# The twelve conditioning chunks of the input stage, computed on VectorE with features on partitions instead of as matrix products on TensorE

## The reference, cut to what matters

```python
# first block, D_MODEL = 1024
sh1, sc1, gt1, sh2, sc2, gt2 = split(silu(c) @ ada_w + ada_b, 6)       # ada_w: 1024 x 6144
csh1, csc1, ...              = split(silu(c_ctx) @ ada_w + ada_b, 6)   # only csh1 and csc1 are used
h = rms_norm(x) * (1 + sc1) + sh1
q, k, v, g, hy_u, gate_ret, gate_hy = split(h @ w_in + b_in)           # w_in: 1024 x 6656
...
# second block, two layers, conditions c_2 and c_ctx_2, ada_w_2: 2 x 1024 x 6144
m = silu(cond) @ ada_w_2[layer] + ada_b_2[layer]
```

## Time and profile before

| what | us |
|---|---|
| median of 3 runs | 1832.39 |
| lowest and highest run | 1829.98, 1832.53 |
| span of the profiled execution | 1829.5 |
| TensorE busy in the span | 1767.4 |
| VectorE busy in the span | 462.7 |

### The profile page before, as it was taken

One profiled execution on the slowest core, in us unless ns is written; L12 is line 12 of the kernel. 1 busy time (PEld: TensorE's weight loads), 2 busy tenths in 40 slices (PEclk: granted clock), 3 DMA queues, 4 the chain that ended last, 5 costly groups with the idle time before them and its releaser, 6 DMA issues. The chain is left out here.

```text
span 1829.5 us, 24606 instructions
## 1 busy us (share of the span) xinstructions
PE 1767.4 (97%) x10866; PEld 1344.7 (73%) x10866; DVE 462.7 (25%) x1010; ACT 324.7 (18%) x732; POOL 0.2 (0%) x4
## 2 busy tenths in 40 slices
PE   6999999999999999999999999999999999999997
PEld 4674887888664466676667577688888876888886
DVE  5310124525125221111101144531100135411001
ACT  4110013103214111010000123521100125211000
POOL 0000000000000000000000000000000000000000
PEclk9999999999999999999999999999999999999999
DMA  9453677467999999999999973365444331554430
GB/s 380 177 224 116 259 316 280 185 253 268 372 391 414 401 421 420 421 421 421 398 421 407 421 291 118 139 241 181 153 161 140 113 116 46 215 200 161 142 111 23
DMA packets 61810, 472.93 MB, mean 259 GB/s; under 512 B 7719, under 2 KB 11208, under 8 KB 12040
## 3 DMA queue, kind: packets, MB, share of 16 engines
q1 hardware_dynamic: 60472, 470.08, 65.7%
q10 hardware_dynamic: 1232, 1.28, 0.2%
HBM read 470.29 MB, written 1.05 MB: 258 GB/s over the span
## 5 line engine op out<-in xcount | busy, mean ns | idle before, releaser
L2520 PE MATMUL bank<-hT,ring 128*128 128x256 f32 x1024 | 221.5, 379 | 0.0
L2539 PE MATMUL bank<-second_work,ring 128*128 128x256 f32 x1024 | 221.3, 379 | 0.0
L2539 PEld LDWEIGHTS bank<-second_work,ring 128*128 128x128 f32 x1024 | 194.6, 190 | 26.5
L2520 PEld LDWEIGHTS bank<-hT,ring 128*128 128x128 f32 x1024 | 194.4, 190 | 26.4
L1345 PE MATMUL bank<-hT,ring 128*128 128x256 f32 x704 | 160.8, 385 | 4.5 <-issue 2.7
L1345 PEld LDWEIGHTS bank<-hT,ring 128*128 128x128 f32 x704 | 133.1, 192 | 39.8 <-issue 12.9
L650 PE MATMUL bank<-hT,ring 128*128 128x256 f32 x704 | 153.9, 379 | 0.0
L650 PEld LDWEIGHTS bank<-hT,ring 128*128 128x128 f32 x704 | 133.5, 191 | 18.8 <-issue 1.2
L1813 PE MATMUL bank<-ring,rowsT 128*32 128x512 f32 x1008 | 117.5, 597 | 1.2 <-DMA ring<-in_expert_w 1.0
L1345 PE MATMUL bank<-tmp,ring 128*128 128x256 f32 x384 | 86.5, 382 | 5.9 <-DMA ring<-in_w_out 4.3
L1345 PEld LDWEIGHTS bank<-tmp,ring 128*128 128x128 f32 x384 | 71.9, 190 | 24.8 <-DMA ring<-in_w_out 7.8
(11 more groups left out here) (468 smaller groups left out, 1707.5 us busy)
## 6 DMA issues: line engine op xcount, KB each, us to landing
ring<-in_expert_w SPq DMA_DIRECT2D x190, 1024.0 KB, 12.2
ring<-in_w_ff SPq DMA_DIRECT2D x96, 1024.0 KB, 7.1
ring<-in_ada_w SPq DMA_DIRECT2D x36, 2048.0 KB, 10.4
ring<-in_w_in SPq DMA_DIRECT2D x29, 1024.0 KB, 8.2
ring<-in_w_in SPq DMA_DIRECT2D x13, 2048.0 KB, 8.8
ring<-in_w_out SPq DMA_DIRECT2D x12, 1024.0 KB, 6.0
ring<-in_ret_w_o SPq DMA_DIRECT2D x2, 2048.0 KB, 8.2
ring<-in_w_out SPq DMA_DIRECT2D x2, 2048.0 KB, 12.8
```

The costliest lines, as they stand in the source:

```text
L2520: mm = pe.matmul(ff_bank(n), w[:, k, (n % 2) * P:(n % 2 + 1) * P], hT[:, k, xs], start=k == 0, stop=k == DT - 1)
L2539: mm = pe.matmul(ff_bank(FT + i), w[:, f, :], W[:, 16 * h + f, :], start=h == f == 0, stop=h == 1 and f == FT // 2 - 1)
```

## The change

The 12 conditioning chunks of the input stage leave TensorE. The host lays their weights out transposed (`rows_first`): a chunk holds 4 groups of 128 output features, the features on the partitions, the 1024 input features along the row; it is still 128 x 4096. The conditions come as rows, broadcast to all partitions by three transfers of 128 x 1024 on SyncE's queue, ahead of `early` and the chunks, and ScalarE takes their silu behind tile 9. One step of `weigh` is a `scalar_tensor_tensor` on VectorE over 128 x 1024: weights times condition, with the sum along the row written to `mod`. A0 to A3 are now the chunks of `mods[2]`, with two conditions, 8 steps each; A4 to A11 are those of `mods[0]`, with one condition, 4 steps each: 64 steps. The steps are spread over the tiles of the projection chunk that comes next in the list, behind that tile's evacuation where VectorE does it. A conditioning chunk is released by its last step. The conditioning chunks also move in the list: the counts behind each projection chunk change from 0 0 1 1 1 1 1 1 2 1 1 1 1 to 0 1 1 1 2 2 1 1 1 1 1 0 0.

```diff
-                  [wide("ada_w", j) for j in range(ADA0, 12)] + [wide("ada_w_2", j, 1) for j in range(4)],
-                  [0, 0, 1, 1, 1, 1, 1, 1, 2, 1, 1, 1, 1])
+                  [features_first("ada_wT", j) if l is None else features_first("ada_wT_2", j) for l, j in ROW_CHUNKS],
+                  [0, 1, 1, 1, 2, 2, 1, 1, 1, 1, 1, 0, 0])
...
+                    cond_rows = {0: row_of(tmp[:, 6:8, :]), 2: row_of(gates[:, 12:16, :]), 3: row_of(tmp[:, 0:2, :])}
+                    products_out = row_of(tmp[:, 2:4, :])
+                    row_jobs = [(c, mods[0], 4 * (ADA0 + j), (0,)) if l is None else (c, mods[2], 4 * j, (2, 3))
+                                for c, (l, j) in zip(at["in_beside"], ROW_CHUNKS)]
+                    row_steps = [(n, i, m) for n, job in enumerate(row_jobs) for i in range(4) for m in range(len(job[3]))]
...
+                    def row_steps_after(i):
+
+                        here = [s for s, (n, _, _) in enumerate(row_steps) if i in tiles_of_next[n]]
+                        if not here:
+                            return range(0)
+                        where = tiles_of_next[row_steps[here[0]][0]]
+                        done = lambda t: here[0] + len(here) * t // len(where)
+                        return range(done(where.index(i)), done(where.index(i) + 1))
+
+                    def weigh(dve, s):
+
+                        n, i, m = row_steps[s]
+                        chunk, mod, first, conds = row_jobs[n]
+                        if i == m == 0:
+                            wait_chunk(dve, chunk)
+                        w = chunk_tile(chunk, D)[:, i, :]
+                        if len(conds) == 2 and s >= 2:
+                            dve.wait_ge(S("weighed"), s - 1)
+                        nc.vector.scalar_tensor_tensor(out=w if m == len(conds) - 1 else products_out, in0=w, scalar=1.0,
+                                                       in1=cond_rows[conds[m]], op0=ALU.mult, op1=ALU.mult,
+                                                       accum_out=mod[:, first + i, m:m + 1]).then_inc(S("weighed"), 1)
...
+                        for s, (n, i, m) in enumerate(row_steps):
+                            freed[row_jobs[n][0]] = (S("weighed"), s + 1)
...
-                                for n in due(i):
-                                    if n == 0:
-                                        pe.wait_ge(S("hy_spec_out"), 4)
-                                    beside.pe(pe, n)
...
+                            for m in (0, 2, 3):
+                                sp.dma_start(cond_rows[m], a["cond_rows"][m:m + 1, :].to_broadcast([P, D]))\
+                                    .then_inc(S("rows_loaded"), 16)
...
-                                for n in due(i):
-                                    beside.dve(dve, n)
...
-                            dve.wait_ge(S("ada_added"), len(ada_jobs))
...
+                                if i == N_KEYS + TT:
+                                    dve.wait_ge(S("cond_rows"), 3)
+                                for s in row_steps_after(i):
+                                    weigh(dve, s)
...
+                            dve.wait_ge(S("weighed"), len(row_steps))
...
+                                    if i == len(tiles) - 4:
+                                        act.wait_ge(S("weighed"), len(row_steps))
...
-                                for n in due(i):
-                                    beside.act(act, n)
+                                if i == N_KEYS + 1:
+                                    act.wait_ge(S("rows_loaded"), 64)
+                                    for m in (0, 2, 3):
+                                        nc.scalar.activation(cond_rows[m], cond_rows[m], ACT.Silu).then_inc(S("cond_rows"), 1)
```

More of the change, by code:

```diff
@@ L122, in build, with features_first @@
         ADA0 = 4
+        ROW_CHUNKS = [(1, j) for j in range(4)] + [(None, j) for j in range(8)]
+        def features_first(name, j):
+            return a[name][j].rearrange("p (i k) -> p i k", k=D)
         plan("ada", [wide("ada_w", j) for j in range(ADA0)])
@@ L429, in four_of, with add_ada_bias @@
             return [(where[n], mod[:, 4 * (first + n):4 * (first + n) + 4, :], pair) for n in range(4)]
-        def add_ada_bias(mod, lo, hi, bias):
-            return nc.vector.tensor_tensor(mod[:, lo:hi, :], mod[:, lo:hi, :],
-                                           bias.rearrange("p (i a) -> p i a", a=1).to_broadcast([P, hi - lo, 2]), ALU.add)
+        def add_ada_bias(mod, lo, hi, bias, n=2):
+            return nc.vector.tensor_tensor(mod[:, lo:hi, 0:n], mod[:, lo:hi, 0:n],
+                                           bias.rearrange("p (i a) -> p i a", a=1).to_broadcast([P, hi - lo, n]), ALU.add)
         def half(b):
@@ L554, in build @@
                                  for i in range(4)]
[L556 to L559, removed]
+                    row_of = lambda x: x.rearrange("p a t -> p (a t)")
@@ L560, in build @@
                     order = [e for e, _ in evac]
                     nb = 4
[L563 to L568, removed]
+                    tiles_of_next = {}
+                    for n, job in enumerate(row_jobs):
+                        follows = min(t[0] for t in tiles if t[0] > job[0])
+                        tiles_of_next[n] = [i for i, t in enumerate(tiles) if t[0] == follows]
@@ L587, in short_conv @@
                         if n == 0:
+                            dve.wait_ge(S("weighed"), row_steps_after(n_hyena - 1)[-1] + 1)
                             all_of(dve, nc.vector.memset(hyT[:, :, 0:1], 0.0),
@@ L2967, in tiles, with rows_first @@
     return w.reshape(*w.shape[:-2], w.shape[-2] * n)
+def rows_first(w):
+    return w.T.reshape(-1, 4, P, D).transpose(0, 2, 1, 3).reshape(-1, P, 4 * D)
 def up_pieces(w):
@@ L3008 @@
         "router_rows": np.concatenate([x["router_expert_b"], x["router_group_b"]], 1).reshape(1, -1),
+        "cond_rows": np.concatenate([x[n].reshape(1, D) for n in ("c", "c_ctx", "c_2", "c_ctx_2")], 0),
+        "ada_wT": rows_first(x["ada_w"][0][:, 2 * D:]), "ada_wT_2": rows_first(x["ada_w_2"][1][:, 0:2 * D]),
         "base": base, "const1": const1, "early": early, "const2": const2, "feats": feats,
@@ L3014 @@
         "rpb": rpb, "sgu_b": sgu_b, "sgu_wT": x["sgu_w_2"].transpose(3, 0, 1, 2),
-        "ada_w": tiles(x["ada_w"][0], NCOLS), "w_in": tiles(x["w_in"][0], NCOLS), "ret_w_o": tiles(x["ret_w_o"][0], NCOLS),
+        "ada_w": tiles(x["ada_w"][0][:, 0:2 * D], NCOLS), "w_in": tiles(x["w_in"][0], NCOLS), "ret_w_o": tiles(x["ret_w_o"][0], NCOLS),
         "hy_w_o": tiles(x["hy_w_o"][0], D), "w_out": tiles(x["w_out"][0], NCOLS),
```

4 lines of the change are left out of this document (2 added, 2 removed).

## The result

| | before | changed | changed, second set |
|---|---|---|---|
| median, us | 1832.39 (5 runs) | 1837.93 (5 runs) | 1837.91 (6 runs) |
| lowest to highest, us | 1829.98 to 1832.71 | 1833.22 to 1843.74 | 1835.15 to 1841.83 |
| ratio to before, 95% interval | | 1.0037 [1.0021, 1.0054] | 1.0039 [1.0025, 1.0053] |
| span of the profiled execution, us | 1829.5 | 1842.0 | 1833.8 |
| next stage's first matmul at, us | 295.98 | 303.45 | 303.67 |

The change makes the kernel slower: the median by 5.5 us, the ratio is 1.0037. The forecast was +12.2 us. The sign and the range held; the forecast was about twice too large. (In the second set the kernel before ran at a median of 1832.03.)

A forecast was written before the change was run, and what follows sets the result against it. TensorE, busy 97% of the span and never waiting in most of the input stage, was taken as the bound. Removed work -26.2, waits +33.0 and clock +5.4 gave +12.2 us: 1844.5 us, range 1836 to 1859.

The forecast's parts named there:

- TensorE's removed work: Input stage: twelve conditioning chunks leave TensorE, saving 26.2 us if TensorE never waits.
- Who releases what: Ring of four chunks: P3 takes A2's slots, P6 A4's, P7 A5's, each released by late steps on VectorE.
- The waits: TensorE waits for loads of P1, P2, P3, P6, P7 and P9, 33.0 us in sum.
- the step: One VectorE multiply over 128x1024 with its row sum: 1.38 us, near ends 1.24 and 1.50.
- the load: A projection chunk's transfer alone: 7.9 us from issue to landing, bounds 7.9 to 8.7 and some wake-up.
- The 0.1 for the wake-up of SyncE: Each wait for a released slot: 0.1 us for SyncE's wake-up before the load.
- The spacing of a pair: Two loads issued close together: the next in line lands 4.95 us behind the first.
- The clock: TensorE restarts at half clock behind the waits for P3, P6 and P7: 1.8 us each, 5.4 in all.
- its end of +26: Slow end of the forecast: 1.50 a step, 3.3 us of clock at four waits, slower landings; 1859 us.
- Rival 1: VectorE steps: the row sum halves the rate, 2.48 us a step, +38, 1870 us; chance 0.10.
- Rival 2: Releases reach SyncE at least 8 us early, so waits for P3, P6, P7 vanish: -22, 1810 us; chance 0.06.
- Rival 3: Waits are short, a load on an otherwise idle queue taking 5.0 us: -2, 1830 us; chance 0.06.

The follow-up runs named there:

- second set: The changed kernel run once more, unaltered, beside the other kernels on one chip: 1837.91 us (6 runs), ratio 1.0039 to the kernel before.
- The kernel with early steps and rows moved: Changed kernel with A2 and A4 finished behind earlier tiles and P1's load issued ahead of the condition rows' transfers: 1806.93 us, ratio 0.9862 to the kernel before.
- the two kernels with releases moved: Changed kernel with only step places altered: one finishing A2 and A4 behind earlier tiles, 1808.13 us; one moving only A2's eight steps earlier, 1824.83 us.

## Why the prediction was right in sign and too large

**TensorE's removed work: right.** Forecast -26.2. The kernel with early steps and rows moved shows it nearly bare: from P0's start (39.76 before, 40.60 there) to the next stage 256.2 before and 230.6 there, 25.6 less with one wait of 0.34 still in it. The stage change is about as taken: the evacuation of the last gate starts at 302.67, the next matmul at 303.45. (By the rows the eleven chunks come to 23.8 and not 23.7; nothing hangs on it.)

**Who releases what: right.** SyncE issued P3's, P6's and P7's loads behind exactly the steps named, and in the two kernels with releases moved just those waits vanished.

**The waits: the step and the load were sized too high.** Forecast 33.0, measured 26.2.

| wait for | forecast | measured | why |
|---|---|---|---|
| P1 | 0.4 | 0.38 | in part luck: 0 to 1.41 in the other executions with this order of transfers |
| P2 | 2.8 | 0.21 | eight steps 9.2 us, not 11.0, begun 0.9 later; TensorE also came 1.2 later |
| P3 | 11.5 | 10.41 | two steps 2.3, not 2.8; load 7.4, not 7.9 |
| P6 | 12.9 | 11.57 | three steps 3.4, not 4.2; load 7.4 |
| P7 | 4.4 | 3.38 | two steps 2.3; load 7.4 |
| P9 | 1.0 | 0.23 | one step 1.15, not 1.38; load 7.4 |

The first mis-sized term is **the step**: 1.38 forecast, 1.145 measured. The larger part, 0.13, is the accumulator's read-out, which was priced like a small operation of its own, 0.14 us. It is an instruction of its own, as the profile shows, but a row of 0.08 us that starts together with the next step and moves its start by 0.01. That it is a second instruction is what the page "VectorE: DVE Perf Modes" of the Trainium skill (Two Vector instructions with no wait between them) has, and the trace agrees. But even the low end without the sum, 1.24, was too high, against 1.135. The working divided the time of a row of operations by their number, and a row's time holds the tail of its last operation: each step is 1.22 us long and starts 1.145 after the one before. The interval is (total - one duration) / (count - 1): for the four operations of 512 columns (2.74 - 0.745) / 3 = 0.665 instead of 0.685, and for the eight of 256 columns, 0.48 long each, 0.397 instead of 0.41. Continued to 1024 columns these give 1.20, so this explains 0.04 of the 0.105; the rest lies in continuing the line from two other operations.

The second term is **the load**: 7.9 from the earlier trace rows, one load. The three loads here that found the queue empty (issued at 149.76, 190.74 and 209.79) took 7.3, 7.3 and 7.4, the first two although another load was issued 0.37 behind them. Why the same 2 MB took 7.9 to 8.8 at such places before was not tried. The 0.1 for the wake-up of SyncE stands on no row; here it issued P3's load 0.03 us behind the end of the last step's read-out. The spacing of a pair was right: A2 and P2, issued 0.37 apart, landed 7.5 and 12.0 us after their issues, 4.9 from one another.

**The clock: right in size.** Forecast 5.4; measured 1.69 + 1.66 + 1.79 = 5.1 in the profile shown, in the later one about 2.3 and 2.0 and 0.1 behind P7's 3.43 us. The forecast expected a slow start behind each of the three waits. P3 and P6 have it; P7 has a drop 1.4 us after its start in one execution and none in the other.

**Left out:** 1.3 us behind P4's start. From there to the marker it is 206.4 us before and 212.5 in the changed kernel, 6.0 more. The waits behind P4 (25.8) and the clock (5.1), less 26.2, make 4.7. A row of matmuls that starts from rest is 0.2 to 0.3 longer than its tiles times their pace (14.08 against 13.8, 27.73 against 27.5), and the waits make five such rows; the prediction counted only the idle time. Together: 12.2 - 6.8 (waits) - 0.3 (clock) + 1.3 = 6.4 against 6.7 measured from P0's start to the marker; the other 0.8 of the marker's 7.5 is P0's later start in this execution. The median of the runs moved by 5.5; the interval of the ratio is 3.9 to 9.9 us (1.0021 and 1.0054 of 1832). It holds 5.3, 6.7 and 7.5 alike. One bound of the prediction doesn't add up: 8.8 instead of 7.9 for five loads is 4.5 more, as its end of +26 has it, and not 6.

**What was expected to be seen:** no conditioning matmuls, the two long waits between 10 and 12 us where they were named, each begun 3.0 and 4.2 us before SyncE's issue, the lower clock behind them: all there. Steps 1.3 to 1.5 us apart and the marker at 308 were not: 1.145 and 303.5.

**Rival 1, the sum halves VectorE:** falls. The step with the sum is 1.145, far below 2, and 1.135 without. The rule of halved throughput from the page "Vector Engine (DVE) Microarchitecture Reference" of the Trainium skill (Points that are easy to get wrong) is not borne out for two float32 sources in SBUF and a 1024-column sum.

**Rival 2, loads not late, 1810:** not what this change did, but its arithmetic is borne out. Where the steps are placed ahead of those tile waits, the kernel takes 1808 and 1807.

**Rival 3, a lone load in 5 us:** falls, with 7.3 to 7.4.

## What to carry to other kernels

Work that is moved to an idle engine is free only as far as nobody waits for its *end*: here 77 us of new VectorE work could be had for nothing, and the place of the last steps of three chunks cost 30. When a consumer of a ring moves to another engine, ask which transfer its release lets go, and have it finish at least one load (7.4 us for 2 MB here) plus the other work behind it before the successor is wanted; steps spread evenly up to the last tile leave the whole load bare. A small net change can be the difference of two large terms (26 saved, 31 lost here), so each of them has to be sized by itself. When costing a row of back-to-back operations from a trace, take start-to-start intervals, not the row's time by its count.

## What the runs showed of the hardware that was not expected

- The sum along a row comes nearly free: DVE_READ_ACCUMULATOR takes 0.08 us, overlaps the next operation, and steps are 1.145 us apart with it and 1.135 without (128x1024, float32, both sources in SBUF).
- Unchanged stretches behind 303 us differ by up to 8 us between executions of one kernel (1530.1 and 1538.5), with granted clocks of 0.99 and 0.95 between 560 and 700 us. One pair of profiles can't decide a few microseconds; a marker at the end of the changed stage can. What sets off these drops was not tried and stays open.
- Behind 3.4 us of idle time TensorE started P7 at 2.4 GHz and fell to 1.2 for about 3 us only some 1.4 us later in one execution of the changed kernel (P7's and P8's row 1.79 us longer), and not at all in the next. Behind 10.4 and 11.6 us it started at 1.2 GHz both times.
- A 2 MB load on an empty queue landed after 7.3 us with another issued 0.37 us behind it; in the kernel before, 8.7 with the next 1.9 us behind the earlier trace rows. What makes the difference stays open.
